# Sums of squares laid between the first products, four raw weight buffers, and a sum over dilations made by the turning matmuls

## The reference, cut to what matters

```python
h = rms_norm(x, norm_g)                       # needs the sum of squares over the 1024 features
dx = token_shift(h) - h
x_r, x_w, x_k, x_v, x_a, x_g = (h + dx * mu[i] for i in range(6))
r = x_r @ w_in[:, c[0]:c[1]]                  # then k, v, g in the same way
```

```python
mix = jax.nn.softmax(jnp.stack(lses, axis=0), axis=0)
o = jnp.einsum('gbsh,gbshd->bshd', mix, jnp.stack(outs, axis=0))      # the sum over three dilations
y_attn = o.reshape(b, s, ATTN_WIDTH).astype(x.dtype) * jax.nn.silu(z_attn)
y = jnp.concatenate([y_conv, y_attn], axis=-1)
x = x + jnp.einsum('bse,ed->bsd', y, w_out)
```

## Time and profile before

| what | us |
|---|---|
| median of 3 runs | 3105.56 (3090.75 to 3108.91) |
| the profiled execution | 3103.45 |
| its span | 3101.6 |
| TensorE busy | 2881.4 (93%) |
| VectorE busy | 1603.5 (52%) |
| ScalarE busy | 1082.7 (35%) |
| GpSimd busy | 619.5 (20%) |

### The profile page before, as it was taken

How to read it: one execution, slowest core, us unless ns; L and a number is a source line. 1 busy time by engine, 2 the same in 40 slices (tenths; PEclk the granted TensorE clock), 3 DMA queues, 4 the chain that set the end, 5 groups by cost and what they waited for, 6 DMA issues and landing times. The chain is left out here.

```text
span 3101.6 us, 77931 instructions
## 1 busy us (share of the span) xinstructions
PE 2881.4 (93%) x34698; PEld 2361.3 (76%) x34698; DVE 1603.5 (52%) x2628; ACT 1082.7 (35%) x2003; POOL 619.5 (20%) x417
## 2 busy tenths in 40 slices
PE   7999999999878888888888999999999999999899
PEld 4887888887467777777787778888877887777677
DVE  5533232432267777777763663222377304777762
ACT  4223332322645445454453441001122113556310
POOL 5522222210023232232321120000000001332320
PEclk9999999999989999999998999999999999999999
DMA  5123331211653232332306763111111226225472
GB/s 174 62 78 116 104 107 48 95 48 57 214 152 98 79 105 74 96 97 78 108 18 191 225 181 83 34 41 41 40 63 62 89 90 232 71 90 180 155 247 85
DMA packets 342221, 326.15 MB, mean 105 GB/s; under 512 B 14159, under 2 KB 254159, under 8 KB 341248
## 3 DMA queue, kind: packets, MB, share of 16 engines
q1 hardware_dynamic: 313296, 261.72, 27.9%
q10 hardware_dynamic: 24480, 47.21, 4.3%
q0 software_dynamic: 4112, 12.25, 1.5%
HBM read 203.18 MB, written 122.64 MB: 105 GB/s over the span
## 5 line engine op out<-in xcount | busy, mean ns | idle before, releaser
L331 PE MATMUL pj_ps<-pj_x_hi,pj_w_hi 128*128 128x512 f32 x1024 | 402.7, 393 | 11.4 <-DVE pj_w_lo L280 6.7
L331 PE MATMUL pj_ps<-pj_x_hi,pj_w_lo 128*128 128x512 f32 x1024 | 400.0, 391 | 0.0
L331 PE MATMUL pj_ps<-pj_x_lo,pj_w_hi 128*128 128x512 f32 x1024 | 400.0, 391 | 0.0
L2017 PE MATMUL dm_ps<-h_hi,dm_w_hi 128*128 128x512 f32 x896 | 279.5, 393 | 0.0
L2017 PE MATMUL dm_ps<-h_hi,dm_w_lo 128*128 128x512 f32 x896 | 275.9, 389 | 0.0
L2017 PE MATMUL dm_ps<-h_lo,dm_w_hi 128*128 128x512 f32 x896 | 275.8, 389 | 0.0
L221 POOL TENSOR_TENSOR pj_x<-h 128x512 f32<-128x512 f32 x128 | 166.9, 1305 | 487.3 <-DVE pj_x_lo L275 438.8
L275 DVE TENSOR_TENSOR pj_x_lo<-pj_x,pj_x_hi 128x512 fp32r<-128x512 f32 x128 | 91.6, 715 | 321.5 <-ACT pj_x_hi L350 321.3
L331 PEld LDWEIGHTS pj_ps<-pj_x_hi,pj_w_hi 128*128 128x128 f32 x1024 | 193.2, 189 | 55.4 <-DVE pj_w_lo L280 9.3
L331 PEld LDWEIGHTS pj_ps<-pj_x_lo,pj_w_hi 128*128 128x128 f32 x1024 | 193.4, 189 | 41.3 <-issue 1.0
L331 PEld LDWEIGHTS pj_ps<-pj_x_hi,pj_w_lo 128*128 128x128 f32 x1024 | 193.2, 189 | 40.5
(11 more groups left out here) (268 smaller groups left out, 5893.4 us busy)
## 6 DMA issues: line engine op xcount, KB each, us to landing
proj<-pj_out ACTq DMA_DIRECT2D x128, 256.0 KB, 2.5
pj_w<-w_in SPq DMA_DIRECT2D x32, 512.0 KB, 4.3
proj<-lr_out SPq DMA_DIRECT2D x32, 512.0 KB, 5.8
dm_w<-w_out SPq DMA_DIRECT2D x32, 512.0 KB, 5.3
dm_w<-w_in SPq DMA_DIRECT2D x30, 512.0 KB, 4.9
partial<-wa_ob SPq DMA_DIRECT2D x48, 264.0 KB, 2.2
mo_part<-partial SPq DMA_DIRECT2D x16, 792.0 KB, 9.1
wa_vt<-v_rows SPq DMA_DIRECT2D x44, 260.0 KB, 3.2
```

The source lines that it names most:

```text
L331: mm = pe.matmul(ps[i][:], wp, xp, start=k == 0 and m == 0, stop=k == KT - 1 and m == len(parts) - 1)
L2017: last = pe.matmul(PS[:, 2 * i + b, :], wp, hp[:, k, t0:t0 + 512], start=k == 0 and m == 0, stop=k == KT - 1 and m == len(parts) - 1)
```

## The change

Three edits:
- In the first stage, the eight sums of quarter 1 no longer stand ahead of the blocks: in the first block (q = 0, r = 0) the sum of k follows the three products of k. The semaphore of the first block is raised with its last product, ahead of the last sum.
- In the last stage, the raw weights go through four buffers; two of them are laid over the six tiles of residual and output (`res`, `out`), which therefore become one tensor `both`. SyncE waits for the window's stores before w3 instead of before the residuals, loads the convolution of block 1 after w5 instead of w3, and waits for all eight splits before the first residual load.
- For the first 512 tokens (b = 0) GpSimd's additions are gone. A turn makes 12 matmuls in transpose mode, for each of four column groups one for each dilation, accumulating in PSUM, and waits for VectorE's product alone. Blocks 1 to 3 keep the additions and the turn of four.

```diff
@@ -330,18 +330,25 @@
                 for m, (wp, xp) in enumerate(parts):
...
                                    stop=k == KT - 1 and m == len(parts) - 1)
-            mm.then_inc(s_mm, 1)
+                if q == 0 and r == 0:
+                    if k == KT - 1:
+                        mm.then_inc(s_mm, 1)
+                    square_sum(1, k)
+            if q or r:
+                mm.then_inc(s_mm, 1)
             if q == 0 and r in (KT - 1, 2 * KT - 1):
...
 
+        def square_sum(b, k):
+            n = b * KT + k
+            pe.wait_ge(s_square, n + 1)
+            pe.matmul(var[b][:], ones[:], sq[n % 2][:], start=k == 0, stop=k == KT - 1).then_inc(s_summed, 1)
+
         pe.wait_ge(s_ones, 2)
-        for b in range(2):
-            for k in range(KT):
-                n = b * KT + k
-                pe.wait_ge(s_square, n + 1)
-                pe.matmul(var[b][:], ones[:], sq[n % 2][:], start=k == 0, stop=k == KT - 1).then_inc(s_summed, 1)
+        for k in range(KT):
+            square_sum(0, k)
         blocks(pe, body)
...
@@ -2602,18 +2609,22 @@
         prod = [sb(f"prod{i}", [128, NG, HEADS, DH]) for i in range(2)]
...
         y2 = [sb(f"y2{i}", [128, CB, 128]) for i in range(2)]
-        res, out = ([sb(f"{n}{i}", [128, 512]) for i in range(RING)] for n in ("res", "out"))
+        both = sb("res_out", [128, 2 * RING, 512])
+        res, out = ([both[:, RING * m + i] for i in range(RING)] for m in range(2))
         part = [sb(f"part{i}", [128, 2, NG, HEADS, DH + 2]) for i in range(2)]
...
         w = [sb(f"w{i}", [128, KT, 128]) for i in range(2)]
+        raw = [w[0][:], w[1][:]]
+        raw += [both[:, i:i + 2].rearrange("p i (k c) -> p (i k) c", c=128) for i in (2, 4)]
+        RAW_OF = (0, 1, 0, 2, 3, 1, 0, 2)
         top, tot, inv = (sb(n, [128, 2, HEADS]) for n in ("top", "tot", "inv"))
...
         turned = [c.enter_context(nc.psum_tensor(f"mo_turned{i}", [128, CB, 128], F32)) for i in range(2)]
-        s_w, s_res, s_out = ([sem(f"{n}{i}") for i in range(k)] for n, k in (("w", 2), ("res", RING), ("out", RING)))
+        s_w, s_res, s_out = ([sem(f"{n}{i}") for i in range(k)] for n, k in (("w", 4), ("res", RING), ("out", RING)))
         s_part = [sem(f"part{i}") for i in range(2)]
...
@@ -2634,9 +2645,10 @@
         @block.sync
...
             def load_w(j):
-                if j >= 2:
-                    sp.wait_ge(s_w_lo, j - 1)
-                sp.dma_start(w[j % 2][:], w_cols[:, :, quarter(j)]).then_inc(s_w[j % 2], 16)
+                before = [i for i in range(j) if RAW_OF[i] == RAW_OF[j]]
+                if before:
+                    sp.wait_ge(s_w_lo, before[-1] + 1)
+                sp.dma_start(raw[RAW_OF[j]], w_cols[:, :, quarter(j)]).then_inc(s_w[RAW_OF[j]], 16)
 
...
@@ -2657,7 +2669,7 @@
 
...
                 if n < NB * KT:
-                    sp.dma_start(res[n % RING][:], res_v[:, n % KT, cols(n // KT)]).then_inc(s_res[n % RING], 16)
+                    sp.dma_start(res[n % RING], res_v[:, n % KT, cols(n // KT)]).then_inc(s_res[n % RING], 16)
 
...
@@ -2675,11 +2687,12 @@
             window_sync(sp, beside)
...
             load_z(0)
+            outputs_stored(sp, NS)
             for j in range(3, KT):
                 load_w(j)
-                if j == 3:
+                if j == 5:
                     load_conv(1)
-            outputs_stored(sp, NS)
+            sp.wait_ge(s_w_lo, KT)
             for n in range(RING):
...
@@ -2690,7 +2703,7 @@
                     if j == 0 and b + 1 < NB:
...
                     sp.wait_ge(s_sum, n + 1)
-                    sp.dma_start(dst_v[:, j, cols(b)], out[n % RING][:]).then_inc(s_out[n % RING], 16)
+                    sp.dma_start(dst_v[:, j, cols(b)], out[n % RING]).then_inc(s_out[n % RING], 16)
                     load_res(n + RING)
...
@@ -2709,17 +2722,17 @@
             for k in range(CB):
...
                 pool.tensor_tensor(y_lo[0][:, k, :], conv[:, k, :], y_hi[0][:, k, :], ALU.subtract).then_inc(s_conv_lo, 1)
-            for n in range(4 * NB):
+            for n in range(4, 4 * NB):
                 pool.wait_ge(s_prod, n + 1)
                 pool.tensor_tensor(prod[n % 2][:, 0], prod[n % 2][:, 0], prod[n % 2][:, 1], ALU.add).then_inc(s_add, 1)
-                pool.wait_ge(s_add, 2 * n + 1)
+                pool.wait_ge(s_add, 2 * (n - 4) + 1)
                 pool.tensor_tensor(prod[n % 2][:, 0], prod[n % 2][:, 0], prod[n % 2][:, 2], ALU.add).then_inc(s_add, 1)
...
                 dve.wait_ge(s_w_hi, j + 1)
-                dve.tensor_tensor(w_lo[j][:], w[j % 2][:], w_hi[j][:], ALU.subtract).then_inc(s_w_lo, 1)
+                dve.tensor_tensor(w_lo[j][:], raw[RAW_OF[j]], w_hi[j][:], ALU.subtract).then_inc(s_w_lo, 1)
 
...
@@ -2784,9 +2797,11 @@
                 n = b * KT + j
...
                 dve.wait_ge(s_res[n % RING], 16 * (n // RING + 1))
+                if n == 0:
+                    dve.wait_ge(s_w_lo, KT)
                 if n >= RING:
                     dve.wait_ge(s_out[n % RING], 16 * (n // RING))
-                dve.tensor_tensor(out[n % RING][:], ps[n % BANKS][:], res[n % RING][:], ALU.add).then_inc(s_sum, 1)
+                dve.tensor_tensor(out[n % RING], ps[n % BANKS][:], res[n % RING], ALU.add).then_inc(s_sum, 1)
 
...
@@ -2874,12 +2889,18 @@
 
...
                 n = 4 * b + i
-                pe.wait_ge(s_add, 2 * n + 2)
+                if b:
+                    pe.wait_ge(s_add, 2 * (n - 4) + 2)
+                else:
+                    pe.wait_ge(s_prod, n + 1)
                 if n >= 2:
                     pe.wait_ge(s_gated, n - 1)
+                groups = range(1 if b else NG)
                 for j in range(CB):
-                    last = pe.transpose(turned[n % 2][:, j, :], prod[n % 2][:, 0, 2 * j:2 * j + 2, :]
-                                        .rearrange("p h d -> p (h d)"), ident)
+                    for g in groups:
+                        last = pe.matmul(turned[n % 2][:, j, :], prod[n % 2][:, g, 2 * j:2 * j + 2, :]
+                                         .rearrange("p h d -> p (h d)"), ident, start=j == 0 and g == 0,
+                                         stop=g == groups[-1], is_transpose=True, skip_group_check=True)
                 last.then_inc(s_turned, 1)
...
@@ -2919,8 +2940,8 @@
         @block.scalar
...
             def weights(j):
-                act.wait_ge(s_w[j % 2], 16 * (j // 2 + 1))
-                act.copy(w_hi[j][:], w[j % 2][:]).then_inc(s_w_hi, 1)
+                act.wait_ge(s_w[RAW_OF[j]], 16 * RAW_OF[:j + 1].count(RAW_OF[j]))
+                act.copy(w_hi[j][:], raw[RAW_OF[j]]).then_inc(s_w_hi, 1)
 
...
```

## The result

The changed kernel takes 3109.17 us (median of 20 runs, 3101.35 to 3122.76), the kernel before 3100.63 in its 20 runs beside them (3090.06 to 3115.3). The medians differ by 8.5 us. The ratio is 1.0026, with a 95% interval of 1.0014 to 1.0039: 4 to 12 us slower, far inside one per cent. The forecast was +3.6 us, slightly slower and no measurable difference at 1%. The profiled execution after has a span of 3110.8 us against 3101.6.

The account below looks back on a forecast made before the run. TensorE is busy 93% of the span, but ScalarE, VectorE and a load set the first restart, and loads of partials and residual the end. 1.4 + 2.2 = +3.6 us on the profiled 3103.45 gave 3107, range 3094 to 3119.

Parts of the forecast that it names:

- Term 1: First stage: sums behind products make ScalarE late and TensorE's restart later, +1.4 us (ends 0 and +3.2).
- cast 2: First stage, ScalarE's cast at 27.29: comes at 28.4, 1.1 us late, behind a square waiting for the first sum.
- the lag after the first sum: First stage, ScalarE: the 1.1 us lag stays, 0.1 is added, and a late square at k = 4 adds about 0.4.
- The upper end (+3.2): First stage: +3.2 us if the clock has fallen in the gap before k = 6 and the last step is slow too.
- Term 2: Last stage: partials land later, so products go on at 2966.7 instead of 2964.53, +2.2 us (ends +1.5 and +4.0).
- upper end of 4.0: Last stage: +4.0 us if the load queue gives back nothing of the partials' late issue.
- The wait at turn 4: Last stage, second half: TensorE stands some 6 us after five groups of products, until GpSimd's sum ends it.
- my walk: Last stage, first 512 tokens: step-by-step times of products and turns, putting the second half at 2921.9 instead of 2925.55.
- Rival 1: Last stage: partials land no later, so the earlier second half counts; -5.5 us, 3099 with the first stage's loss; chance 0.24.
- Rival 2: First stage: the square ring runs at TensorE's pace, about +11 us, 3117 in all; chance 0.12.
- Rival 3: Last stage: turns cool TensorE's clock, the last turn before the second half ends about 4 us later, 3111; chance 0.12.
- Rival 4: Last stage: accumulating turns cost 0.24 us a matmul, 1.6 more for each of four, partials 6 us later, 3113; chance 0.08.

Follow-up runs that it names:

- e3: The changed kernel with SyncE issuing the partials of tokens 512 on before its wait for all eight splits; ratio to the kernel before 0.9987 (0.9969 to 1.0004).

## Why the prediction was right

**The mechanism was right in both stretches, the sizes were low in both.** Forecast 1.4 + 2.2 = 3.6 us. Measured in the profiles 2.0 + 4.1 = 6.1, and 8.5 (4 to 12) in the timing. That the time itself, 3109.17, lies only 2 us from the 3107 that I named is partly luck: the 3107 stood on a single execution of 3103.45, and the kernel before has a median of 3100.63 in its 20 runs.

**Term 1, the beginning: forecast +1.4, measured +2.0 (pacing alone +1.7, the changed kernel with the partials moved +2.8).** The kernel before has the shortest stretch of the nine that don't put products first; against their mean of 37.3 the three are 1.4, 1.7 and 2.5 longer. The steps held: cast 2 late by 1.3 (forecast 1.1), the weight cast at k = 4 behind a late square (35.65, where it was 32.57), the slack of 2.19 used up, the restart behind the same instructions, 7 us of idle TensorE (forecast 8). The step that was too small is the lag after the first sum, "0.1 added" and "about 0.4". Two slow steps made a second square wait, 1.33 us, and the later ones still 0.41 and 0.66, so the casts of k = 6 and 7 came 2.1 late, not 1.6. The upper end (+3.2) covers it.

**Term 2, the last stage: forecast +2.2, measured +4.1, just over the upper end of 4.0.** (Against the mean of the three untouched stages, 201.2, it is 4.8.) Held: a turn of twelve takes 1.33 us in the chain of waits (forecast 1.3); the gap before products 5 is 1.92; SyncE's partials after the eighth split; the end hanging on the partials. The wait at turn 4 was 5.32, where I said some 6; my own figures give 7.0 (2942.5 - 2935.5). The five groups ahead of turn 4 took 15.5 us (44.7 - 29.2) and not five times 2.7, as they start slow after the gap; before they had taken 15.3 (2940.88 - 2925.55). That was overlooked and cost nothing, as it fell into the wait. Two sizes failed that count. The first is the arrival of w3. What I wrote of the stores' wait, "which makes it a little later; z is ahead of it in the queue, which hides that", held: w3 was issued at 3.3 after the first product (2902.61), where it had been 3.0 (2897.39). But I left its landing time as it was. ScalarE waited for w3 until 2909.45:

```profile
2909.45 1.05 ACT L2944 CAST mo_w_hi<-mo_res_out 128x1024 fp32r<-128x1024 f32 x1 [7.72 <-DMA mo_res_out<-w_out]
```

that is 10.1 us after the first product and not 8.3 as before (2902.63). The issues of w3 before, then of w3 and w4 after, with us to landing:

```profile
mo_w<-w_out SPq DMA_DIRECT2D x1, 512.0 KB, 5.2
...
mo_res_out<-w_out SPq DMA_DIRECT2D x1, 512.0 KB, 6.8
...
mo_res_out<-w_out SPq DMA_DIRECT2D x1, 512.0 KB, 8.2
```

w3 took 6.8 us from issue to landing, where it had taken 5.2 with the convolution behind it. So the products of j = 3 waited 0.94 us, which my walk did not have; the 0.94 ahead of j = 4 was in it, as 1.0. Turn 3 ended at 27.1 after the first product instead of my 25.4: 0.9 of it is that wait, the rest 0.2 to 0.3 us in each of the next steps. The partial load was issued at 33.6 instead of 32.1. The second is the landing: 7.83 us, where I had taken 7.5. With 1.5 and 0.3 us, 2.2 becomes 4.0, against 4.1 measured, closer than the scatter of 1.5 warrants. Part of w3's lateness is scatter. With SyncE's old order w3 took 5.1 to 6.2 us to land over seven kernels, with the new one 6.0 to 6.8 over five, so the two executions compared here are near the two ends. On the whole w3 lands later in the new order; whether that comes from the loads right behind it isn't shown, as no kernel changed only that.

**Rivals.** Rival 1 (the earlier second half counts) asked for partials that land in time; with the change they don't, and e3 shows that the rival's mechanism is real where they do. (Its better end is 3098 by its own terms, 3103.45 - 5.5, and not 3097.) Rival 2 (the ring at TensorE's pace) did not come: after 31 us the sums fit. Rival 3 (turns cool TensorE) did not come: the rows show no clock lost through the turns. The windows view of both kernels over the same piece of the stage (columns as in the earlier trace rows), first before (its second row is the last of the earlier trace rows) and then after:

```profile
2910.00:2925.00 15.00, 8.88 (x34) 6.51 (x32) 7.91 (x8) 2.77 (x5) 3.96 (x3) 0.89 0.39 114
```

```profile
2915.00:2930.00 15.00, 10.11 (x52) 8.27 (x53) 6.43 (x9) 3.13 (x4) 0.00 (x0) 0.95 0.17 42
2930.00:2935.00 5.00, 5.00 (x20) 4.02 (x18) 1.10 (x1) 0.00 (x0) 0.00 (x0) 0.81 0.51 137
```

Before, the granted clock was 0.89 and 0.68 around the start of the second half, and after, 0.95 and 0.81. The rule of the Trainium skill that the transpose mode doesn't count as busy ("TensorE: Matmul & The Clock Gate", Part 4: PE-mode transpose) would have made that stretch cooler, with 16 more turning matmuls in it (turns 2 and 3); these rows don't show it. They don't exclude it either, since TensorE's longest gap in this piece fell from 2.59 to 2.16 us. Rival 4 fell with 1.33 us a turn.

**What the sum hid.** Turns and wait stood in one term of 2.2 us. Measured apart they are -3.4 and +7.1. Both signs were in the working (the second half 3.7 earlier, the partials 4.0 later), but they met at turn 4, where only the later one counts; as two terms they would have shown that one can be had without the other.

## What to carry to other kernels

When buffers are laid over each other, the price is the wait that guards them, and it falls on everything queued behind it on the issuing engine, also on loads that don't touch these buffers. So put the wait directly ahead of the transfers that need it, and issue the others first. And where accumulation steps are laid between other work, put the one that another engine waits for ahead of the filler, not behind it.

## What the runs showed that I had not expected

- Untouched stages vary more than the change: the start of the last stage lay between 2888.2 and 2901.0 us over the profiles, without relation to the edits. Single spans can't be compared at this size; of the stretches within a profile the first repeats to 0.7 us (37.0 to 37.7 for the nine profiles with unpaced or sum-first beginnings), the last to 1.5 (200.4 to 201.9 for three profiles).
- A turn of four took 1.11 us to its end instead of 0.60 to 0.66 after an idle time of 5.32 (at 2949.32 after the change; the same with SyncE's wait alone, after 6.77). The length of the rest isn't what tells: after the change the next turn but one took 1.05 after 2.44 idle (2962.45), and before one took 0.66 after 2.61 (2953.47). The granted clock tells: 0.65 over the three us around the turn at 2949.32, 0.61 over 2962.4 to 2963.2, and 0.92 over 2953.4 to 2954.2 before.
- Loads of 512 KB issued in a row behind a 1 MB load (w3 and w4 behind z): 6.8 and 8.2 us to landing. Before, w3 behind z and with a 1 MB load after it took 5.2, and a later load of weights alone 3.9. Over all kernels w3 lay between 5.1 and 6.8.
